# Opening of a two-layer encoder: where the ones-products, the norm's broadcast and the first modulation columns stand

## The reference, cut to what matters

```python
def _rmsnorm(x, g):
    y = xf * lax.rsqrt(jnp.mean(xf * xf, axis=-1, keepdims=True) + EPS)
    return y * g
def _modulation(c, w_mod, b_mod):
    m = jax.nn.silu(c) @ w_mod + b_mod
    shift, scale, gate = jnp.split(m, 3, axis=-1)
for i in range(2):
    shift, scale, gate = _modulation(c, w_mod[i], b_mod[i])
    h = _rmsnorm(x, norm_g[i]) * (1.0 + scale) + shift
    y = _short_conv_mixer(h, ...) if i == 0 else _spatial_gating_mixer(h, ...)
    x = x + gate * y
return _rmsnorm(x, final_g)
```

## Time and profile before

| | us |
|---|---|
| median of 3 runs | 830.36 |
| lowest, highest | 830.31, 832.19 |
| profiled execution | 830.13 |
| its span | 827.9 |
| TensorE busy in the span | 804.7 |
| VectorE busy | 645.9 |
| ScalarE busy | 438.7 |

### The profile page before, as it was taken

How to read it: one execution, slowest core, us unless ns; L and a number is a source line. 1 busy time by engine, 2 the same in 40 slices (tenths; PEclk the granted TensorE clock), 3 DMA queues, 4 the chain that set the end, 5 groups by cost and what they waited for, 6 DMA issues and landing times.

```text
span 827.9 us, 15170 instructions
## 1 busy us (share of the span) xinstructions
PE 804.7 (97%) x5590; PEld 750.8 (91%) x5590; DVE 645.9 (78%) x942; ACT 438.7 (53%) x616; POOL 52.0 (6%) x64
## 2 busy tenths in 40 slices
PE   6999999999999999999999999999999999989996
PEld 5779999999999999978889888899999999878896
DVE  5989999998998989888534676488888888867534
ACT  4575656666665565543224833356766667842210
POOL 1010000000001000000000000010000000000000
PEclk9999999999999999999999999999999999999999
DMA  9894565656666666587321352424454555494103
GB/s 350 343 251 134 148 194 169 208 163 204 174 181 177 183 178 200 149 344 273 116 80 67 109 200 85 125 74 128 128 149 134 148 152 139 137 356 156 51 1 102
DMA packets 39501, 137.84 MB, mean 166 GB/s; under 512 B 4272, under 2 KB 6448, under 8 KB 39472
## 3 DMA queue, kind: packets, MB, share of 16 engines
q1 hardware_dynamic: 32128, 111.16, 36.5%
q0 software_dynamic: 6912, 25.17, 16.2%
q10 hardware_dynamic: 432, 1.13, 0.3%
HBM read 108.09 MB, written 4.19 MB: 136 GB/s over the span
## 4 chain that ended last, share of the span: by engine, by line
PE 89%; DVE 5%; ACT 3%; issue 2%; DMA 1%; SPq 0%; ACTq 0%; DVEq 0%
PE pp L1109 10%; PE pp L1110 10%; PE pp L1111 10%; PE pp L974 8%; PE pp L975 8%; PE pp L976 7%; PE p_aux L1109 7%; PE p_aux L1111 6%; PE p_aux L1110 6%; PE pp L1245 4%; PE pp L1246 4%; PE pp L1247 4%; PE p_aux L1319 2%; DVE acc_s L1405 1%; PE pp L1064 1%
## 5 line engine op out<-in xcount | busy, mean ns | idle before, releaser
L1109 PE MATMUL pp<-h_hi,wh 128*128 128x256 f32 x280 | 79.3, 283 | 0.0
L1111 PE MATMUL pp<-h_hi,wl 128*128 128x256 f32 x280 | 79.2, 283 | 0.0
L1110 PE MATMUL pp<-h_lo,wh 128*128 128x256 f32 x280 | 79.2, 283 | 0.0
L1610 DVE TENSOR_TENSOR wl<-wt,wh 128x1024 fp32r<-128x1024 f32 x56 | 66.5, 1219 | 0.2 <-ACT wh L647 0.2
L647 ACT ACTIVATE wh<-wt 128x1024 fp32r<-128x1024 f32 x56 | 58.9, 1054 | 13.7 <-DVE wt L1591 7.6
L1109 PE MATMUL pp<-s_hi,wh 128*128 128x256 f32 x224 | 63.4, 283 | 0.0
L1110 PE MATMUL pp<-s_lo,wh 128*128 128x256 f32 x224 | 63.4, 283 | 0.0
L1111 PE MATMUL pp<-s_hi,wl 128*128 128x256 f32 x224 | 63.4, 283 | 0.0
L1111 PE MATMUL p_aux<-s_hi,wl 128*128 128x256 f32 x224 | 63.4, 283 | 0.0
L1110 PE MATMUL p_aux<-s_lo,wh 128*128 128x256 f32 x224 | 63.4, 283 | 0.0
L1109 PE MATMUL p_aux<-s_hi,wh 128*128 128x256 f32 x224 | 63.4, 283 | 0.0
(11 more groups left out here) (223 smaller groups left out, 2589.5 us busy)
## 6 DMA issues: line engine op xcount, KB each, us to landing
raw<-in_stream SPq DMA_DIRECT2D x144, 512.0 KB, 4.0
wl<-raw POOLq DMA_DIRECT2D x28, 512.0 KB, 4.6
raw_l<-in_stream SPq DMA_DIRECT2D x18, 512.0 KB, 8.9
raw_s<-in_stream SPq DMA_DIRECT2D x16, 512.0 KB, 13.6
wl_b<-raw POOLq DMA_DIRECT2D x16, 512.0 KB, 4.5
raw_m<-in_stream SPq DMA_DIRECT2D x14, 512.0 KB, 3.2
x_s<-in_xt SPq DMA_DIRECT2D x4, 512.0 KB, 6.0
w_lo_s<-raw POOLq DMA_DIRECT2D x4, 512.0 KB, 5.6
```

What stands on the lines that cost most here:

```text
L1109: pe.matmul(out, hi, hi_of(k), start=fresh and k == 0, stop=False, skip_group_check=not fresh)
L1110: pe.matmul(out, hi, lo_of(k), start=False, stop=False, skip_group_check=not fresh)
L1111: mm = pe.matmul(out, lo, hi_of(k), start=False, stop=k == 3, skip_group_check=not fresh)
L1610: dve.tensor_tensor(wl[par][:, part], wt[par][:, part], f32(wh[par][:, part]), ALU.subtract).then_inc(t_cut, 1)
```

## The change

Four edits, all in the opening. TensorE's wait for the first square goes, so that its ones-products depend on the constants alone. They become 24 instead of 6. On TensorE broadcast goes ahead of start_columns(0). On VectorE the wait for broadcast and the scaling of tile 0 go ahead of start_amp(0), and the scaling of tile 1 stays behind it; scale_tile is the body of scale_pair.

```diff
-WARM = (6, 2)
+WARM = (24, 2)
...
             pe.wait_ge(consts, 3)
-            pe.wait_ge(sq_ready, 1)
             keep_clock(WARM[0])
...
             direct_columns(0, 1)
+            broadcast(p_rstd[:, :], 2, ALL)
             start_columns(0)
-            broadcast(p_rstd[:, :], 2, ALL)
             pe.wait_ge(amp_ready, 1)
             direct_columns(1, 0)
             keep_clock(WARM[1])
...
                 for k in (2 * kp, 2 * kp + 1):
-                    dve.tensor_tensor(staged(layer, k, where), (x if layer else x_s)[:, k, where], scale,
-                                      ALU.mult).then_inc(h_scaled, 1)
+                    scale_tile(k, scale, where, layer)
+
+            def scale_tile(k, scale, where, layer):
+
+                dve.tensor_tensor(staged(layer, k, where), (x if layer else x_s)[:, k, where], scale,
+                                  ALU.mult).then_inc(h_scaled, 1)
...
+            dve.wait_ge(rstd_bc, 1)
+            scale_tile(0, p_rstd[:, :], ALL, 0)
             start_amp(0)
-            dve.wait_ge(rstd_bc, 1)
-            scale_pair(0, p_rstd[:, :], ALL, 0)
+            scale_tile(1, p_rstd[:, :], ALL, 0)
             cut_lo_start(0)
```

## The result

| | before | after |
|---|---|---|
| median of 9 runs | 830.31 us | 833.47 us |
| lowest, highest | 830.02, 832.48 | 831.99, 837.61 |
| profiled execution | 830.13 | 834.92 |
| its span | 827.9 | 832.7 |

The ratio after to before is 1.0039, with a 95% interval of 1.0022 to 1.0055: slower by 3.2 us in the medians, and outside the predicted range. The profiled executions lie 4.8 us apart. This is TensorE's timeline of the opening of the changed kernel; its lines answer to the earlier trace rows.

The account below looks back on a forecast made before the run. TensorE was taken to bound the kernel, with VectorE tighter after the first block. A 1.0 us earlier variance, amp 0.84 us later and slack summed to +0.2 us: 830.5 for a median, range 828.6 to 832.3.

Parts of the forecast that it names:

- Part 1: Opening: 24 ones-products end at 10.7, direct_columns(0, 0) takes about 1.9 us, variance comes 1.0 us earlier, diagonals at 16.93.
- part 2: Broadcast ahead of start_columns(0): start_columns ends at 19.01 and amp is ready at 19.47, 0.84 us later.
- part 3: TensorE's direct_columns(1, 0) waits for amp until about 19.57; first block's products start at 21.72 instead of 21.13.
- Part 4: Slack ahead of the h_lo group takes up loss: amp at 28.23 moves by +0.2, bounds 0.0 and +0.35.
- rival A: Opening: the ones-products don't bring the clock; products start at 22.73, +1.2 us, 831.5; chance 0.12.
- rival B: Opening: clock falls in two new TensorE waits, 1.7 us lost, 832.2 (two falls 833.9); chance 0.06.
- far below that ahead of 727: Argument against a clock fall in the opening: its idle share is far below that ahead of the fall at 728.
- it slides by the same amount, and so does the end: VectorE's queue from 28.23 to 51.35, and the end, shift by as much as the amp at 28.23.
- The part that said what else moves: SyncE's next loads are issued up to 1.8 us earlier; the chain from 23.44 names no transfer, so nothing is counted.
- from 51.35 it is TensorE alone: Reading of the chain behind the opening: from 51.35 us on only TensorE holds it.
- Rival C: Opening's late clock rise, or the fall at 728, is avoided by the change: 828.6 to 829.5; chance 0.20.
- two of three runs and the profiled one lie within 0.23 us: Argument against a clock rise that often comes later than 14.4 in the kernel before.

Follow-up runs that it names:

- e5: The changed kernel with ScalarE's two loads of 512 KB (ws and bs) issued some 20 us later: 830.17 us, ratio 0.9979.
- e7: The changed kernel with its opening pauses filled (32 ones-products first, six ahead of broadcast, two ahead of the wait for amp): 833.61 us, ratio 1.0019.
- e13: The changed kernel with the 24 ones-products of 128 columns made as six of 512 columns: 831.60 us, ratio 1.0004.
- e1: The changed kernel with six ones-products and the wait for the first square as before, only the order changed: 831.53 us, ratio 1.0012.
- e3: The changed kernel with six more ones-products between direct_columns(0, 1) and broadcast: 834.04 us, ratio 1.0031.
- e10: The changed kernel with ScalarE's two loads some 20 us later and VectorE's release of x_updated earlier: 827.40 us.
- e14: The changed kernel, unchanged, profiled a second time: 833.65 us, ratio 1.0029.
- e11: e10 with the opening's pauses filled by ones-products as in e7: 826.55 us.
- e2: The kernel before with 24 ones-products from the constants on, the order as before: 835.43 us, ratio 1.0046.
- e8: The kernel before with 14 ones-products meant for the pause at 723 us in the second out product, but put behind it: 834.25 us, ratio 1.0030.
- e15: The kernel before, unchanged, profiled a second time: 832.15 us in its one run.
- e6: The kernel before with ScalarE's two loads (ws and bs) some 20 us later: 830.62 us, ratio 0.9984.
- e9: The kernel before with ScalarE's two loads some 20 us later and VectorE's release of x_updated earlier: 826.23 us.
- e16: e11 with ones-products of 512 columns where there are four or more: 826.44 us, ratio 0.9948 to the kernel before.
- e12: e2 with ScalarE's two loads some 20 us later and VectorE's release of x_updated earlier: 827.33 us.

## Why the prediction was wrong

**Right from 10.8 us on, step by step: TensorE's queue.** Part 1 gave variance at 14.45 (measured 14.42) and the diagonals at 16.9 (17.03); part 2 amp at 19.47 (19.45); part 3 direct_columns(1, 0) at 19.57 (19.51) and the products at 21.72, which e5, e7 and e13 show where the clock holds (21.58, 21.65, 21.62). Part 4's +0.2 is -0.1 to 0.0 in these three (28.13, 28.20 and 28.18 against 28.23), just under its bounds of 0.0 and +0.35. e1 alone costs +1.0 at the second amp, near the +1.2 of rival A.

**First step that failed: the end of the ones-products, and with it the chance of rival B.** The mechanism was named, two waits on TensorE and a fall, and priced at 1.7 us; the opening lost 1.6. But it got 0.06, on the ground that the idle share lay "far below that ahead of 727". That one row shows a fall behind a pause of 3.86 us says nothing of shorter pauses. And the forecast counted two pauses, because part 1 let the products end at 10.7, as the slot lands. Six profiles have these three pauses or, in e3, the first and the last:

| | clock rose at | ones-products end | pauses | fall |
|---|---|---|---|---|
| after | 5.7 | 9.20 | 1.57, 1.60, 0.52 | 19.35 |
| e10 | 5.6 | 9.16 | 1.49, 1.60, 0.52 | 19.25 |
| e3 | 4.6 | 8.66 | 2.02, filled, 0.51 | 11.4 |
| e14 | 7.7 | 10.15 | 0.82, 1.60, 0.52 | none |
| e5 | 7.5 | 10.09 | 0.51, 1.61, 0.52 | none |
| e13 | 7.9 | 10.17 | 0.49, 1.60, 0.51 | none |

Where the rise came near the 7.7 of part 1, the products ended 0.5 us early and the clock held; where it came 2 us sooner, they ended 1.5 us early and the clock fell. With an early rise it held only where the pauses were filled (e7, e11) or the second was 0.72 us (e2). So 24 products are too few for an early rise, and the fall was about as likely as not: three of the six. Whether it takes the long first pause, or the early rise in some other way, these runs can't separate.

**Second: "it slides by the same amount, and so does the end".** This carried the sum from 28.23 to the end and it is where the range broke: 3.3 us came in at 370. The part that said what else moves looked at SyncE's loads in the opening and at a chain that names no transfer. It left out that 18 more products are 18 more sets of TensorE's instructions, and that these come through the same DMA engines. The slot that they delayed had made VectorE wait 0.5 us already in the kernel before, and TensorE 0.8 us for the y_lo behind it. The reading "from 51.35 it is TensorE alone" passed over that: rows 3 end at 62 us, and in rows 1 11% of the chain isn't TensorE's.

**Rival C was right on the kernel before.** Its opening, in five profiles, has the second amp at 27.95, 28.23, 30.08, 30.18 and 33.47 (e8, before, e15, e6, e9) as the clock rises at 14.1 to 27.0 us. The 29 runs of the kernel before beside e13 to e16 stand in groups that answer to it: 19 from 829.2 to 830.8, three near 832.4, four near 834.9, and three near 831.3. These three have no profile, but a mean granted clock of 0.994 where the other 26 have 0.997, so they probably had a fall more, rather than a late rise, which that mean doesn't count. The text gave it 0.20, which is near the seven in 29; but the median doesn't see what happens in a quarter of the runs, while the change's own losses are in most of them. The change does what it was for, direct_columns(0, 0) at the higher level in five of the six profiles above, and none of these has its second amp later than 30.91.

**How far the moment of the rise varies.** The Trainium skill (TensorE: Matmul & The Clock Gate, Part 1, "What's actually happening") says that the moment of the rise varies from run to run of one kernel. The five profiles agree, 14.1 to 27.0 us. I had weighed it down by "two of three runs and the profiled one lie within 0.23 us"; four runs were too few to see a case of one in four.

**Open.** Why the packet's place varies between 12.8 and 9.9 in two executions of the same kernel (after, e14) wasn't tried, nor was how much of the late slots' wait is the packet itself and how much its order in the queues. How the parts share the median's 3.2 us is known for the two profiles only; for the other executions of the changed kernel, 19 with e14's, only the lower mean granted clock shows that all of them had low stretches in addition.

## What to carry to other kernels

Ones-products that keep the clock must reach up to the work that they are for, and a reorder that opens a pause of a us or two on TensorE puts that clock at stake again: fill the pause, or price the fall at the chance with which the profiles show it (here three of six). Make them few and wide, since each instruction is also code that has to be fetched through full DMA queues, and a stage with a transfer that is just in time can pay for it hundreds of us later. Before saying that a shift slides through to the end, look for the waits on transfers that are under a us now, not only at the chain. And before taking a mechanism from one profile, compare it with the clock and time of all executions.

## What the runs showed of the hardware

- One packet of TensorE's code (16 KB, about 1.1 us of one DMA engine) among loads of 512 KB that keep all 16 engines full goes with a slot landing 0.9 to 1.9 us late, in six profiles of six. With 1 MB of another queue moved away from there VectorE didn't wait for either slot in e10, and 1.3 us for the first in e5.
- The place of that packet moved from 14.0 to 14.5 us behind a load to 9.3 to 12.8 when the list had 18 or more products of 128 columns in addition, ahead of it by 340 us (e13 against e2, e3, e5, e7, e10, e11, e12, e14 and after).
- The clock's granted level fell behind pauses of 1.6, 1.6 and 0.5 us (after), 2.0 us (e3), 1.9 us (e12), 2.4 us (after, at 374), and stayed low for 3.4 us or twice that (49.8 to 56.6 in e2). It held behind 0.5 to 0.8, 1.6 and 0.5 us in e5, e13 and e14.
- In the opening of the kernel before the rise came at 14.1, 14.6, 18.8, 19.0 and 27.0 us, in five executions of the same TensorE list up to there. In the longer list of ones-products from 1.7 us on it came between 4.5 and 7.9.
- PEclk stands at 1.00 in the slices ahead of the first rise (as from 11 to 13 us in the kernel before), although direct_columns(0, 0) runs there at half pace, 3.74 us against 2.02: the durations of the matmuls tell the level there, not the column.
